# Modulation weights as 256 rows by 1024 columns, columns made by transposes, and low weights signalled in pieces

## The chip, the cores and the metric

The kernel runs on one core of one Trainium2 chip. The metric is the device time of one execution in microseconds (us). Engines are named as in the profile: PE is TensorE, DVE VectorE, ACT ScalarE, POOL GpSimd, SP SyncE, whose queue issues the loads of weights.

## The reference

The program is the whole forward pass of a trunk of two layers on 384 tokens: 128 tokens of a prompt and 256 latent tokens, each a vector of 1024 features. Layer 0 mixes tokens with HGRN2 and mLSTM, layer 1 with windowed attention and latent attention (MLA); each layer ends in a SwiGLU network with 2816 hidden features. All of it is fp32. Every layer is modulated by a condition: one vector for the prompt tokens (`c_ctx`) and one for the latent ones (`c`).

```python
def adaln(cond, w, b):
    m = jax.nn.silu(cond) @ w + b          # w: 1024 x 6144
    ...
    return jnp.split(m, 6, axis=-1)        # six vectors of 1024

for l in range(DEPTH):                     # once for the prompt with c_ctx, once for the latent tokens with c
    sh1, sc1, g1, sh2, sc2, g2 = adaln(cond, ada_w[l], ada_b[l])
    h = rms_norm(x, norm1_g[l]) * (1.0 + sc1) + sh1
    x = x + g1 * mixer(h)
    h = rms_norm(x, norm2_g[l]) * (1.0 + sc2) + sh2
    x = x + g2 * ((silu(h @ ffn_w1[l]) * (h @ ffn_w3[l])) @ ffn_w2[l])
```

The change is about the product with `ada_w`: two layers of 1024 x 6144 weights, 50.3 MB of the 162.43 MB that the kernel reads, for only two condition vectors. It gives twelve vectors of 1024 values.

## The kernel before

Activations lie with features on the 128 partitions, in eight tiles, and 384 tokens along the free axis. Every weight matrix is cut into units of up to 1 MB by `plan_units`. SP loads them in that order into a ring of three slots (`raw`, RAW=3): before the load of unit u it waits until unit u-3 is released. A unit of an ordinary matrix is then split into a high and a low part: ACT writes `w_hi` (L1084, up to 2048 columns in one instruction) and POOL writes `w_lo = raw - w_hi` (L1060, pieces of 512 columns), two buffers of each. POOL signals `lo_ready` once for a unit. PE then makes three products for each k-tile, high by high, low by high and high by low (L434 to L436 in `three`, L474 to L476 in `tokens`), 24 for an output tile of 1024 input features. `features` makes one output tile, `first_features` two at a time while the normalised input comes in tile by tile (`h_ready`).

Units of `ada_w` are not split. There are 48 of them, each all eight k-tiles by 256 columns; two make a pair of 512 columns, and there are 24 pairs. PE sums a unit in `strips` (L508): four strips of 32 partitions of a PSUM bank, strip g with k-tiles g and g+4. When both units of a pair are in, DVE copies 128x512 from PSUM (L1506, `ada_row`), PE's `columns_to` (L521) makes columns of it with four small matmuls against the constant `strips`, which also add up the four strips, and DVE adds the bias (L1494). The banks are a ring of two (`adas`). Columns of a pair are made by PE when the next pair has been summed.

Where the pairs are summed is written out by hand in `ADA_PLACES`: four at the start, one in the levels stage of HGRN2 (place norm0, in two halves at j=9 and j=10), one ahead of mLSTM (hgrn_norm), four in mLSTM behind steps j=0 to 3, one ahead of mLSTM's norm, one in norm1 ahead of layer 0's FFN, ten in that FFN (loaded by ACT's queue into a buffer of its own, `vada_raw`), one in norm2, one in norm3. In a norm, DVE's `norm(n, base, place)` writes the tiles `ht` (L1533), and at tile 0 it takes the pair of that place, so that it waits for PE's strips there.

In the levels stage (j = 6 to 17) PE makes one unit of `in0` for each j, and `level` products (L633) behind it. In cq, in layer 1, PE turns the cache with `turn(misc, ("cache",), ...)` and waits on `cq_ready` for the query compression that DVE splits (`cq_lo`), then multiplies by uq.

Of the kernel before, what the change touches and what calls it, by code (L numbers as in the profile page):

```python
# [56 lines left out]
for _name, _k in (("ident", 128), ("ones", 128), ("strips", 2), ("levels", 8 * 128),  # L57
                  ("tri_f", 128), ("tri_b", 128), ("big_f", 128), ("big_b", 128)):
    CONSTS[_name] = (_n, _k)
    _n += _k  # L60
# [8 lines left out]
def shape_constants():  # L69
# [9 lines left out]
    put("strips", np.tile(np.eye(32, 2, dtype=np.float32), (4, 1)))  # L79
    pos = np.arange(TL)  # L80
    rows, cols = (pos // 64).astype(np.float32), (pos % 64).astype(np.float32)
    for name, d, n in (("swa", 64, 2), ("mla", 32, 4)):
# [4 lines left out]
        for a, at in ((0, rows), (1, cols)):  # L87
# [4 lines left out]
            for i in range(half):  # L92
# [33 lines left out]
def ada_pairs(place):  # L126

    at = 0
    for name, n in ADA_PLACES.items():
        if name == place:  # L130
            return range(at, at + n)
        at += n
    raise KeyError(place)


def plan_units():
# [31 lines left out]
    add("in1", 1, DT, 160, 5)  # L168
    add("uq", 2, 3, 384)
# [3 lines left out]
    add("up1", 2, DT, 256)  # L173
    ada("norm3")
    add("up1", FT - 2, DT, 256, 2)
# [4 lines left out]
def build(nc, I, O):  # L180
# [9 lines left out]
    with ctx:  # L190
# [17 lines left out]
        ada_row = sb("ada_row", [P, 2, 512])  # L208
# [169 lines left out]
        first_vada = ada_pairs("ffn0")[0]  # L378
# [38 lines left out]
        vada_at_up = {3 * q + 5: q for q in range(VADA_UP // 2)}  # L417
        vada_at_down = {min(2 * q + 2, DT - 1): VADA_UP // 2 + q for q in range((VADA - VADA_UP) // 2)}

        @block.tensor  # L420
        def _(pe):
            def raw_unit(u):

                pe.wait_ge(raw_in[u % RAW], raw_need[u])
                return raw[u % RAW][:, 0:2048].rearrange("p (k n) -> p k n", k=DT)

# [12 lines left out]
            def unit_ready(u):  # L439
                pe.wait_ge(S["lo_ready"], split_index[u] + 1)  # L440

            def features(key, u, c, k_tiles=DT, x=(h_hi, h_lo), n=T):

                out = dense.fill(pe, key)[:, 0:n]
                unit_ready(u)
                three(out, [(*weight(u, k_tiles, k, c), x[0][:, k, 0:n], x[1][:, k, 0:n]) for k in range(k_tiles)])\
                    .then_inc(dense.done, 1)
                release[u] = (dense.done, dense.at[key] + 1)

            def first_features(keys, u, ready):  # L450

                outs = [dense.fill(pe, key)[:, 0:T] for key in keys]
                unit_ready(u)
                for k in range(DT):
                    pe.wait_ge(S["h_ready"], ready + k + 1)
# [6 lines left out]
            def tokens(key, u, c, n, chunk, k_tiles=DT, x=(h_hi, h_lo), out=None, more=False, last=True):  # L462
# [3 lines left out]
                unit_ready(u)  # L466
# [6 lines left out]
                for j, (s_hi, s_lo, m_hi, m_lo) in enumerate(terms):  # L473
                    pe.matmul(bk[:, at:at + n], s_hi, m_hi, start=j == 0, stop=False)  # L474
# [15 lines left out]
            def vada_half(n):  # L490

                p = first_vada + n // 2
                if n % 2 == 0:
                    vada_out[0] = adas.fill(pe, ("ada", p))
                pe.wait_ge(vada_in[n % 2], 16 * (n // 2 + 1))
                mm = strips(vada_out[0], n % 2, vada_raw[:, n % 2, :].rearrange("p (k n) -> p k n", k=DT))
                if n % 2:
# [3 lines left out]

            vada_out = [None]

            def strips(out, i, w):

                for k in range(DT):
                    g = k % 4
# [1508 lines left out]
```

## Time and profile before

| | |
|---|---|
| three runs | 1201.55, 1201.96 and 1206.5 us (median 1201.96) |
| profiled execution | 1202.52 us, its span 1200.7 us, mean granted clock of PE 0.953 |
| PE, DVE, ACT, POOL busy | 1110.2, 437.6, 399.0, 541.8 us |
| waits of PE's modulation strips on `ada_w` loads | 27.5 us in 13 waits |
| read from HBM | 162.43 MB, 138 GB/s over the span |

The times in the views are microseconds from the start of the span, those in the groups nanoseconds where they are means. Busy is the time in which an engine executes; the chain is followed back from the last instruction, at each step to what released it, so a row in it is time that the end waited for. A pipelined matmul shows some 0.34 us although the next one starts 0.17 us behind it.

### The profile page before, as it was taken

The numbers are of one execution on the slowest core, as the hardware profiler recorded it, in microseconds if no ns is written. First come the engines' busy times: TensorE is split into PE (matmuls) and PEld (weight loads), VectorE is DVE, ScalarE is ACT, GpSimd is POOL, SyncE is SP. The second block draws the span as 40 slices with busy tenths as digits, with TensorE's granted clock in tenths as the row PEclk, the third lists the DMA queues.
The fourth block names the chain that finished last, engine by engine and source line by source line (L and its number), as shares of the span: only waits on it lengthen the run. The fifth ranks groups of instructions, "written<-read, shape, count | busy, mean of one in ns | idle before, by whom it ended". The sixth has DMA issues, their size and how long they took to land.

```text
span 1200.7 us, 17368 instructions
## 1 busy us (share of the span) xinstructions
PE 1110.2 (92%) x7181; PEld 1022.6 (85%) x7181; DVE 437.6 (36%) x886; ACT 399.0 (33%) x617; POOL 541.8 (45%) x422
## 2 busy tenths in 40 slices
PE   5799999978789999999999799779998999999997
PEld 3599999966679999999999698655697999999997
DVE  4647899138563111111112310457465111111122
ACT  0532332434234322223212333456424232332221
POOL 0355478350063555554555433211053656565662
PEclk9799999979799999999999899879998999999998
DMA  9633443458336666664667711231034444534441
GB/s 309 198 108 106 142 141 105 151 180 284 88 117 176 199 195 191 176 185 131 196 188 199 229 42 38 67 86 51 1 103 128 121 135 110 141 98 135 122 121 53
DMA packets 243018, 166.47 MB, mean 139 GB/s; under 512 B 20269, under 2 KB 241532, under 8 KB 242812
## 3 DMA queue, kind: packets, MB, share of 16 engines
q1 hardware_dynamic: 214880, 135.74, 39.2%
q10 hardware_dynamic: 28060, 29.63, 7.8%
q8 instruction: 57, 0.93, 0.3%
q14 instruction: 21, 0.17, 0.0%
HBM read 162.43 MB, written 2.92 MB: 138 GB/s over the span
## 4 chain that ended last, share of the span: by engine, by line
PE 78%; DVE 7%; DMA 5%; POOL 3%; ACT 3%; issue 1%; ACTq 0%; SPq 0%; DVEq 0%
PE banks L434 20%; PE banks L436 20%; PE banks L435 20%; DMA raw<-in_ada_w 4%; PE banks L508 3%; POOL w_lo L1060 3%; PE banks L474 2%; PE banks L475 2%; PE banks L476 2%; DVE ht L1533 2%; PE banks L633 2%; DVE h_lo L1524 2%; ACT w_hi L1084 1%; PE banks L521 1%; PE banks L487 1%
## 5 line engine op out<-in xcount | busy, mean ns | idle before, releaser
L1060 POOL TENSOR_TENSOR w_lo<-raw,w_hi 128x512 fp32r<-128x512 f32 (+2 forms) x410 | 535.0, 1336 | 630.0 <-ACT w_hi L1084 629.9
L434 PE MATMUL banks<-h_hi,w_hi 128*128 128x384 f32 x1088 | 373.8, 344 | 20.7 <-DVE h_lo L1524 11.5
L435 PE MATMUL banks<-h_lo,w_hi 128*128 128x384 f32 x1088 | 368.3, 339 | 0.0
L436 PE MATMUL banks<-h_hi,w_lo 128*128 128x384 f32 x1088 | 368.3, 339 | 0.0
L1084 ACT ACTIVATE w_hi<-raw 128x2048 fp32r<-128x2048 f32 (+4 forms) x115 | 193.5, 1683 | 244.1 <-PE banks L436 172.1
L434 PEld LDWEIGHTS banks<-h_hi,w_hi 128*128 128x128 f32 x1088 | 207.4, 191 | 33.0 <-issue 29.3
L435 PEld LDWEIGHTS banks<-h_lo,w_hi 128*128 128x128 f32 x1088 | 207.6, 191 | 0.6
L436 PEld LDWEIGHTS banks<-h_hi,w_lo 128*128 128x128 f32 x1088 | 207.1, 190 | 0.6
L1587 DVE TENSOR_TENSOR uf<-sa,banks 128x384 f32<-128x384 f32 x44 | 24.4, 554 | 330.2 <-PE banks L436 324.3
L434 PE MATMUL banks<-u_hi,w_hi 128*128 128x384 f32 x352 | 119.8, 340 | 1.0 <-POOL w_lo L1060 1.0
L436 PE MATMUL banks<-u_hi,w_lo 128*128 128x384 f32 x352 | 118.3, 336 | 0.0
L435 PE MATMUL banks<-u_lo,w_hi 128*128 128x384 f32 x352 | 118.3, 336 | 0.0
L1571 DVE SCALAR_TENSOR_TENSOR X<-banks,mod,X 128x128 f32<-128x128 f32 x64 | 23.8, 413 | 193.9 <-PE banks L436 193.8
L1148 ACT ACTIVATE u_hi<-uf 128x384 fp32r<-128x384 f32 x44 | 23.1, 525 | 183.8 <-DVE uf L1587 183.8
L434 PEld LDWEIGHTS banks<-u_hi,w_hi 128*128 128x128 f32 x352 | 66.2, 188 | 4.5 <-issue 2.9
L435 PEld LDWEIGHTS banks<-u_lo,w_hi 128*128 128x128 f32 x352 | 66.2, 188 | 0.0
L436 PEld LDWEIGHTS banks<-u_hi,w_lo 128*128 128x128 f32 x352 | 66.2, 188 | 0.0
L508 PE MATMUL banks<-raw,cond 128*32 128x256 f32 x448 | 36.8, 461 | 27.5 <-DMA raw<-in_ada_w 27.5
L474 PE MATMUL banks<-w_hi,h_hi 128*128 128x256 f32 (+1 forms) x216 | 61.3, 284 | 0.0
L475 PE MATMUL banks<-w_lo,h_hi 128*128 128x256 f32 (+1 forms) x216 | 60.9, 282 | 0.0
L476 PE MATMUL banks<-w_hi,h_lo 128*128 128x256 f32 (+1 forms) x216 | 60.9, 282 | 0.0
L508 PEld LDWEIGHTS banks<-raw,cond 128*32 128x32 f32 x448 | 13.7, 124 | 45.2 <-DMA raw<-in_ada_w 28.4
(311 smaller groups left out, 1204.5 us busy)
## 6 DMA issues: line engine op xcount, KB each, us to landing
raw<-in_ffn_w SPq DMA_DIRECT2D x88, 512.0 KB, 5.2
raw<-in_ada_w SPq DMA_DIRECT2D x28, 1024.0 KB, 7.3
raw<-in_ffn_w SPq DMA_DIRECT2D x32, 704.0 KB, 4.6
vada_raw<-in_ada_w ACTq DMA_DIRECT2D x20, 1024.0 KB, 6.6
raw<-in_w_in_even SPq DMA_DIRECT2D x18, 1024.0 KB, 5.3
raw<-in_w_out_even SPq DMA_DIRECT2D x4, 1024.0 KB, 5.5
raw<-in_w_in_odd SPq DMA_DIRECT2D x3, 1024.0 KB, 7.2
raw<-in_w_in_odd SPq DMA_DIRECT2D x8, 256.0 KB, 4.3
```

The costliest lines, as they stand in the source:

```text
L434: pe.matmul(out, s_hi, m_hi, start=first and j == 0, stop=False)
L435: pe.matmul(out, s_hi, m_lo, start=False, stop=False)
L436: mm = pe.matmul(out, s_lo, m_hi, start=False, stop=last and j == len(terms) - 1)
L474: pe.matmul(bk[:, at:at + n], s_hi, m_hi, start=j == 0, stop=False)
L475: pe.matmul(bk[:, at:at + n], s_hi, m_lo, start=False, stop=False)
L476: mm = pe.matmul(bk[:, at:at + n], s_lo, m_hi, start=False, stop=j == k_tiles - 1)
L508: mm = pe.matmul(out[32 * g:32 * g + 32, 256 * i:256 * i + 256], cond[:, k, :], w[:, k, :], start=i == 0 and k < 4, stop=k >= 4, skip_grou ...
L633: mm = pe.matmul(out[:, h * P:(h + 1) * P], k_side[:, h, c * P:(c + 1) * P], q_side[:, h, c * P:(c + 1) * P], start=h == 0, stop=h == H - ...
L1060: ins = pool.tensor_tensor(w_lo[s % SPLIT][:, at:to], raw[u % RAW][:, at:to], w_hi[s % SPLIT][:, at:to].bitcast(F32), ALU.subtract)
L1084: act.activation(w_hi[s % SPLIT][:, 0:n], raw[u % RAW][:, 0:n], ACT.Copy)\
L1524: ins = dve.scalar_tensor_tensor(h_lo[:, m, a:b], ht[:, m % 2, a:b], mod[:, l, 8 * k + m, c:c + 1], h_hi[:, m, a:b].bitcast(F32), ALU.add, ...
L1587: dve.tensor_tensor(uf[:, f % 2, :], sa[:, f % 2, :], bk[:, 0:T], ALU.mult)\
```

## The change

A unit of `ada_w` becomes 256 rows by 1024 columns, that is two k-tiles by a whole vector; it has rows of 4 KB in memory where it had rows of 1 KB. Four units make a vector. Strip g now sums the columns 256 g to 256 g + 255 over all eight k-tiles, so no strips are left to be added: DVE copies 128x256, two transposes make columns (32 per strip, of which two are used), and one DVE instruction adds the bias to sixteen values. The constant `strips` goes.

POOL raises `lo_ready` behind every piece. `unit_ready(u, k)` makes PE wait for as many pieces as k-tile k needs, when more are needed than it has already seen; SP waits for the count of the whole unit.

Places are counted in units. The pair ahead of mLSTM moves into levels, which then has four units at j=9 to 12 and completes a vector. The vector that norm2 begins is completed in a new place cq, between the turned cache and the wait on `cq_ready`; norm3 has no units any more, and norm2 no longer holds up DVE. The columns of the last mLSTM vector are made before the strips of mlstm_norm.

```diff
-ADA_PLACES = {"start": 4, "norm0": 1, "hgrn_norm": 1, "mlstm": 4, "mlstm_norm": 1, "norm1": 1, "ffn0": 10,
-              "norm2": 1, "norm3": 1}
-assert sum(ADA_PLACES.values()) == 24
-VADA, VADA_UP = 2 * ADA_PLACES["ffn0"], 12
+ADA_PLACES = {"start": 8, "levels": 4, "mlstm": 8, "mlstm_norm": 2, "norm1": 2, "ffn0": 20, "norm2": 2, "cq": 2}
+assert sum(ADA_PLACES.values()) == 48
+VADA, VADA_UP = ADA_PLACES["ffn0"], 12
...
-    def ada(place, pairs=None):
-        units.extend((f"ada{p // 12}", 2 * (p % 12) + i, DT, 256)
-                     for p in (ada_pairs(place) if pairs is None else pairs) for i in range(2))
-    ada("start", range(0, 3))
+    def ada(place, first=0, end=None):
+        units.extend((f"ada{n // 24}", n % 24, 2, 1024) for n in ada_units(place)[first:end])
+    ada("start", 0, 6)
     add("in0", 1, DT, 256)
-    ada("start", range(3, 4))
+    ada("start", 6)
     add("in0", 6, DT, 256, 1)
     add("gates", 1, DT, 16)
-    first, second = [(f"ada{p // 12}", 2 * (p % 12) + i, DT, 256) for p in ada_pairs("norm0") for i in range(2)]
     add("in0", 2, DT, 256, 7)
-    units.append(first)
-    add("in0", 1, DT, 256, 9)
-    units.append(second)
-    add("in0", 8, DT, 256, 10)
+    for i in range(4):
+        ada("levels", i, i + 1)
+        add("in0", 1, DT, 256, 9 + i)
+    add("in0", 5, DT, 256, 13)
     add("out0", 2, DT, 256)
-    for place in ("hgrn_norm", "mlstm", "mlstm_norm"):
+    for place in ("mlstm", "mlstm_norm"):
...
+    ada("cq")
...
-    ada("norm3")
...
+        vada_at_up = {f + 1: n // 4 for f, n in VADA_AT_UP.items() if n % 4 == 3}
+        vada_at_down = {min(m + 1, DT - 1): n // 4 for m, n in VADA_AT_DOWN.items() if n % 4 == 3}
+        lo_need = [0]
+        for u in split_units:
+            lo_need.append(lo_need[-1] + (units[u][2] * units[u][3] + 511) // 512)
...
-            def unit_ready(u):
-                pe.wait_ge(S["lo_ready"], split_index[u] + 1)
+            lo_seen = [0]
+            def unit_ready(u, k=None):
+                s, n = split_index[u], units[u][3]
+                need = lo_need[s + 1] if k is None else lo_need[s] + (n * (k + 1) + 511) // 512
+                if need > lo_seen[0]:
+                    pe.wait_ge(S["lo_ready"], need)
+                    lo_seen[0] = need
             def features(key, u, c, k_tiles=DT, x=(h_hi, h_lo), n=T):
                 out = dense.fill(pe, key)[:, 0:n]
-                unit_ready(u)
-                three(out, [(*weight(u, k_tiles, k, c), x[0][:, k, 0:n], x[1][:, k, 0:n]) for k in range(k_tiles)])\
-                    .then_inc(dense.done, 1)
+                for k in range(k_tiles):
+                    unit_ready(u, k)
...
+            def strips(out, i, w):
+                for k in range(2):
+                    for g in range(4):
+                        mm = pe.matmul(out[32 * g:32 * g + 32, 0:256], cond[:, 2 * i + k, :], w[:, k, 256 * g:256 * g + 256],
+                                       start=i == 0 and k == 0, stop=i == 3 and k == 1, skip_group_check=True)
+                return mm
...
                     out = adas.fill(pe, ("mod", p))
                     adas.was_read(pe, ("ada", p))
-                    for j in range(4):
-                        mm = pe.matmul(out[:, 2 * j:2 * j + 2], ada_row[:, p % 2, j * P:j * P + P], cst("strips"),
-                                       start=j == 0, stop=True, skip_group_check=True)
-                    mm.then_inc(adas.done, 1)
+                    for j in range(2):
+                        tr = pe.transpose(out[:, j * P:j * P + P], ada_row[:, p % 2, j * P:j * P + P], ident)
+                    tr.then_inc(adas.done, 1)
...
+            def modulation(place, first=0, end=None, between=None):
+                for n in ada_units(place)[first:end]:
+                    u = number[(f"ada{n // 24}", n % 24)]
+                    pe.wait_ge(raw_in[u % RAW], raw_need[u])
+                    mm = strips(ada_bank(n), n % 4, raw[u % RAW][:, 0:2048].rearrange("p (k n) -> p k n", k=2))
+                    if n % 4 < 3:
+                        mark(mm, ("ada", n))
+                        release[u] = (S["half_used"], marks[("ada", n)])
+                    else:
+                        mm.then_inc(adas.done, 1)
+                        release[u] = (adas.done, adas.at[("ada", n // 4)] + 1)
+                        columns_to(n // 4)
+                    if between is not None:
+                        between()
+                        between = None
...
-                        columns_to(first_vada if l == 0 else 24)
+                        columns_to(first_vada if l == 0 else 12)
...
             for j in range(6, 18):
-                if j in (9, 10):
-                    modulation_half(ada_pairs("norm0")[0], j - 9)
+                if 9 <= j < 13:
+                    modulation("levels", j - 9, j - 8)
...
-            modulation("hgrn_norm")
...
-                modulation("mlstm", ada_pairs("mlstm")[j:j + 1])
+                modulation("mlstm", 2 * j, 2 * j + 2)
                 for i in TURN_HEADS.get(j, ()):
                     turn_head(i)
+            columns_to(5)
             modulation("mlstm_norm")
...
+            modulation("cq")
             pe.wait_ge(S["cq_ready"], 3)
...
-            modulation("norm3", between=lambda: stat(3))
+            stat(3)
...
-                        sp.wait_ge(S["lo_ready"], split_index[last] + 1)
+                        sp.wait_ge(S["lo_ready"], lo_need[split_index[last] + 1])
...
+                elif name[:3] == "ada":
+                    pieces_of = [(dst, k_first(w[name])[:, i % 4 * 2:i % 4 * 2 + 2, i // 4 * D:i // 4 * D + D])]
...
-                ins.then_inc(S["lo_ready"], 1)
+                    ins.then_inc(S["lo_ready"], 1)
...
-                    dve.tensor_tensor(mod[:, l, t:t + 4, :], bk[:, 0:8].rearrange("p (j c) -> p j c", c=2),
-                                      ada_b_col[:, 48 * l + t:48 * l + t + 4].unsqueeze(2).to_broadcast([P, 4, 2]),
+                    dve.tensor_tensor(mod[:, l, t:t + 8, :].rearrange("p (g j) c -> p j g c", j=2),
+                                      bk[:, 0:256].rearrange("p (j g w) -> p j g w", j=2, g=4)[:, :, :, 0:2],
+                                      ada_b_col[:, 48 * l + t:48 * l + t + 8].rearrange("p (g j) -> p j g", j=2)
+                                      .unsqueeze(3).to_broadcast([P, 2, 4, 2]),
                                       ALU.add).then_inc(adas.read(("mod", p)), 1)
...
+            def take_rows(p):
+                bk = adas.filled(dve, ("ada", p))
+                if ("mod", p - 2) in adas.at:
+                    adas.filled(dve, ("mod", p - 2))
+                dve.tensor_copy(ada_row[:, p % 2, :], bk[:, 0:256]).then_inc(adas.read(("ada", p)), 1)
+                biases_to(p)
+            def modulation(place, first=0, end=None):
+                for n in ada_units(place)[first:end]:
+                    if n % 4 == 3:
+                        take_rows(n // 4)
...
-                    if place is not None:
-                        modulation(place, ada_pairs(place)[m:m + 1])
+                    if place is not None and m == 0:
+                        modulation(place)
...
+            biases_to(5)
             gains(1)
...
-            norm(2, 24, "norm2")
+            norm(2, 24, None)
...
             rope(5)
+            modulation("cq")
...
-            norm(3, 32, "norm3")
+            norm(3, 32, None)
```

## Rows read from the trace of the kernel before

**Rows 1.** The page, chain that ended last: shares of the span by engine.
```profile
PE 78%; DVE 7%; DMA 5%; POOL 3%; ACT 3%; issue 1%; ACTq 0%; SPq 0%; DVEq 0%
```

**Rows 2.** Waits of PE: line, released by: us in total, times, longest.
```profile
PE banks L508 <- DMA raw<-in_ada_w: 27.5, 13, 8.0
...
PE banks L434 <- POOL w_lo L1060: 6.5, 5, 4.3
...
PE banks L434 <- DVE cq_lo L1924: 3.5, 1, 3.5
```

**Rows 3.** Groups by shape: busy us, mean ns | idle before, releasers.
```profile
L434 PE MATMUL banks<-u_hi,w_hi 128*128 128x384 f32 x352 | 119.8, 340 | 1.0 <-POOL w_lo L1060 1.0
...
L521 PE MATMUL banks<-const,ada_row 128*128 128x2 f32 x192 | 26.2, 259 | 1.6 <-DVE ada_row L1506 1.6
...
L1506 DVE COPY ada_row<-banks 128x512 f32<-128x512 f32 x24 | 16.5, 689 | 35.5 <-PE banks L508 26.7 <-issue 7.4 <-DVE PX L1827 0.7
```

**Rows 4.** Chain in order of time, the start: start us, us, what.
```profile
21.73 5.71 DMA raw<-in_ada_w
...
29.47 7.87 DMA raw<-in_ada_w
...
38.46 2.41 PE banks L521 x16
...
54.65 4.96 POOL w_lo L1060 x4
```

**Rows 5.** Windows: busy by engine, granted clock, DMA share, GB/s.
```profile
10.00:15.00 5.00, 2.25 (x20) 0.60 (x16) 0.69 (x1) 0.00 (x0) 0.00 (x0) 1.00 1.04 389
30.00:35.00 5.00, 4.44 (x14) 2.53 (x18) 2.58 (x6) 3.34 (x3) 1.39 (x2) 0.50 1.10 349
280.00:285.00 5.00, 3.75 (x46) 2.90 (x39) 3.12 (x12) 1.00 (x3) 0.00 (x0) 1.00 1.09 350
```

**Rows 6.** GpSimd's groups by shape, 150 to 205 us, then 360 to 660.
```profile
L1060 POOL TENSOR_TENSOR w_lo<-raw,w_hi 128x512 fp32r<-128x512 f32 x21 | 45.1, 2178 | 19.3 <-ACT w_hi L1084 19.2
...
L1060 POOL TENSOR_TENSOR w_lo<-raw,w_hi 128x512 fp32r<-128x512 f32 x111 | 140.5, 1295 | 147.6 <-ACT w_hi L1084 147.6
```

**Rows 7.** Chain in order of time, levels stage.
```profile
144.42 1.00 PE banks L508 x16
...
179.59 2.68 PE banks L633 x24
191.03 2.68 PE banks L633 x24
```

**Rows 8.** Chain in order of time, mLSTM stage.
```profile
268.99 6.50 DMA raw<-in_ada_w
...
280.32 7.98 DMA raw<-in_ada_w
...
290.40 1.06 PE banks L487 x9
...
306.36 3.43 PE banks L508 x32
```

**Rows 9.** Chain in order of time, FFN of layer 0 and norm2.
```profile
373.68 1.91 ACT w_hi L1084
...
416.74 0.79 PE banks L521 x8
...
671.98 9.24 DMA raw<-in_ada_w
...
685.04 0.75 DVE ht L1533 x2
```

**Rows 10.** Timeline of PE at the first down products.
```profile
573.60 0.44 PE L434 MATMUL banks<-u_hi,w_hi 128*128 128x384 f32 x1 [0.57 <-POOL w_lo L1060]
573.88 0.34 PE L435 MATMUL banks<-u_lo,w_hi 128*128 128x384 f32 x1
574.06 0.34 PE L436 MATMUL banks<-u_hi,w_lo 128*128 128x384 f32 x1
```

More of the change, by code:

```diff
@@ L56 @@
 _n = 0
-for _name, _k in (("ident", 128), ("ones", 128), ("strips", 2), ("levels", 8 * 128),
+for _name, _k in (("ident", 128), ("ones", 128), ("levels", 8 * 128),
                   ("tri_f", 128), ("tri_b", 128), ("big_f", 128), ("big_b", 128)):
@@ L78, in shape_constants @@
     put("ones", np.ones((P, P), np.float32))
-    put("strips", np.tile(np.eye(32, 2, dtype=np.float32), (4, 1)))
     pos = np.arange(TL)
@@ L500, in vada_half @@
                     mm.then_inc(S["vada_half"], 1)
[L502 to L507, printed above, removed]
-                    mm = pe.matmul(out[32 * g:32 * g + 32, 256 * i:256 * i + 256], cond[:, k, :], w[:, k, :],
-                                   start=i == 0 and k < 4, stop=k >= 4, skip_group_check=True)
-                return mm
             columns_made = [0]
@@ L602, in _ @@
             misc.was_read(pe, "cond")
-            modulation("start", range(0, 1))
+            modulation("start", 0, 2)
             pe.wait_ge(S["x_in"], 32)
@@ L615, in _ @@
             pe.matmul(out[:, 0:32], ones[0:1, :], row_in[:, :], start=True, stop=True).then_inc(misc.done, 1)
-            modulation("start", range(1, 3))
+            modulation("start", 2, 6)
             stat(0)
-            modulation("start", range(3, 4))
-            columns_to(4)
+            modulation("start", 6)
+            columns_to(2)
             in0 = lambda c: (number[("in0", c // 256)], c % 256)
@@ L892, in scores @@
                     pe.wait_ge(S["roped"], 8)
-                    adas.was_read(pe, ("ada", ada_pairs("norm2")[-1]))
+                    adas.was_read(pe, ("ada", 11))
                     dense.was_read(pe, ("vm", 3))
@@ L1498, in biases_to @@
                     biases_made[0] += 1
-            def modulation(place, pairs=None):
-                for p in (ada_pairs(place) if pairs is None else pairs):
-                    bk = adas.filled(dve, ("ada", p))
-                    if ("mod", p - 2) in adas.at:
-                        adas.filled(dve, ("mod", p - 2))
-                    dve.tensor_copy(ada_row[:, p % 2, :], bk[:, :]).then_inc(adas.read(("ada", p)), 1)
-                    biases_to(p)
+            def take_rows(p):
[6 more added lines that the diff above has]
+                for n in ada_units(place)[first:end]:
+                    if n % 4 == 3:
+                        take_rows(n // 4)
             def gains(n):
@@ L1591, in ffn @@
                     if l == 0:
-                        if f in VADA_AT_UP and VADA_AT_UP[f] % 2:
-                            p = first_vada + VADA_AT_UP[f] // 2
-                            modulation("ffn0", range(p, p + 1))
+                        if f in VADA_AT_UP and VADA_AT_UP[f] % 4 == 3:
+                            take_rows(first_vada + VADA_AT_UP[f] // 4)
                         if f in vada_at_up:
@@ L1605, in ffn @@
                         take_y(m - 1)
-                    if l == 0 and VADA_AT_DOWN[m] % 2:
-                        p = first_vada + VADA_AT_DOWN[m] // 2
-                        modulation("ffn0", range(p, p + 1))
+                    if l == 0 and VADA_AT_DOWN[m] % 4 == 3:
+                        take_rows(first_vada + VADA_AT_DOWN[m] // 4)
                     if l == 0 and m in vada_at_down:
@@ L1615, in _ @@
             dve.memset(cond[:, :, :], 0.0).then_inc(S["cond_clear"], 1)
-            modulation("start", range(0, 1))
+            modulation("start", 0, 2)
             for c in range(NCH):
@@ L1629, in _ @@
             step(dve.tensor_scalar(neg_sink[:, :], rowb[:, 0:8], -1.0, None, ALU.mult))
-            modulation("start", range(1, 2))
+            modulation("start", 2, 4)
             dense.was_read(dve, ("x", NCH - 1, 1))
@@ L1633, in _ @@
                 add_squares(0, m)
-            modulation("start", range(2, 4))
-            biases_to(4)
+            modulation("start", 4)
+            biases_to(2)
             gains(0)
@@ L1771, in _ @@
                 ins.then_inc(misc.read(("kv", 2 + d)), 1)
-            modulation("norm0")
+            modulation("levels")
             bk = dense.filled(dve, "m_cols")
@@ L1860, in _ @@
             weights(0)
-            modulation("hgrn_norm")
             dve.wait_ge(S["hg_sq"], 1)
@@ L1869, in _ @@
                 finish(j)
-                modulation("mlstm", ada_pairs("mlstm")[j:j + 1])
+                modulation("mlstm", 2 * j, 2 * j + 2)
                 if j == 0:
```

91 lines of the change are left out of this document (31 added, 60 removed).

## The prediction

> **What bounds the kernel now.** I read the page's chain that ended last first: the matrix engine holds 78 % of it, VectorE 7 %, DMA 5 %, GpSimd and ScalarE 3 % each, so a change pays where it takes matmuls off TensorE's stream or ends one of its waits [rows 1]. The waits of PE say which are within reach of this diff: 27.5 us of the modulation strips (L508) wait on loads of `ada_w`, the largest wait of all, 6.5 us of feature matmuls on `w_lo`, in five waits, and 3.5 us at one place on `cq_lo` [rows 2]. Then the groups by shape give the price of each small operation [rows 3], and the chain in order of time shows which of these waits ended last in each stage [rows 4, 7 to 9]. Elsewhere PE streams fp32r matmuls 0.17 us apart [rows 10], and only work taken out of the stream counts there.
>
> **The sum**, stage by stage, against the profiled execution (1202.5 us, 1.8 above its span, 0.5 above the median of the runs).
>
> *Start.* Eight strip units are still loaded and summed. What changes: the chain ends its modulation with 16 column matmuls of 2.41 us [rows 4]; of these two vectors leave four transposes, half of which can run earlier. A transpose in the stream costs about 0.12 us at the full clock (nine in 1.06 us [rows 8]), double at the halved clock that is granted here (0.50 [rows 5]): I take 0.7 for what is left, -1.7; bounds -1.2 and -2.1. The loads of 5.71 and 7.87 us are chain [rows 4], at 349 GB/s; the same engines moved the 4 KB rows of the input tokens at 389 [rows 5]. If rows of 4 KB do that here too, 13.6 us of loads lose 10 %, -1.3 (bounds 0 and -1.4). Together **-3.0** (-1.2 to -3.5).
>
> Here a rule of the Trainium skill speaks against the last step. "DMA: Bandwidth & Descriptors", section Specifications, puts the least size for the line rate at 512 B and the HBM's share of a core near 358 GB/s: by it rows of 1 KB lose nothing against rows of 4 KB, and the 349 would already be the limit. The 389 of this trace disagrees, though the token rows follow one another in memory and the new pieces do not; it is rival C.
>
> *Second unit of in0.* PE stood still 4.3 us, its longest wait on `w_lo` [rows 2], while GpSimd made four pieces in 4.96 us [rows 4]. The signal now comes a piece (1.24 us) at a time, and a piece holds two k-tiles of a column tile: six matmuls, 6 x 0.174 = 1.04 us. PE therefore runs at GpSimd's pace and ends its first 24 matmuls one piece's work (1.04) behind the last piece instead of 24 x 0.174 = 4.18 behind it: -3.1, and at best the whole standstill goes, -4.3. I stay near the pace: **-3.5**.
>
> *Levels (j = 6 to 17).* Two units at j=9 and 10 become four at j=9 to 12. Two more strip units are 2 x 1.00 us in the stream [rows 7]. Worse is the ring of three `raw` slots: unit u waits for the release of u-3, so the load of in0's unit 11, which stood behind a split unit and could start early, now stands behind the strips of j=10, and unit 12's, which stood behind those, behind the strips of j=11. From there it is serial: load about 6 us (5.71 and 6.50 at other places [rows 4, 8]), `w_hi` 1.91 [rows 9], then four pieces. A piece takes 2.18 us here against 1.295 in the FFN [rows 6], so 8.7 us for the unit. PE's step of j is 11.44 us (from one `level` product to the next [rows 7]). The last piece lands 6 + 1.9 + 8.7 = 16.6 after the strips; PE wants it a step later, for the last quarter of its first 24 matmuls, 11.44 + 0.75 x 4.18 = 14.6: 2 us late if pieces take their mean, 4 if they take 2.7, once; the next unit then meets PE's delayed pace. Pieces give back about 1 us of the wait for a whole unit. **+4.5** (+2, strips alone, to +8, if the lateness comes at both units). Cover for the first part is only PE's own step.
>
> *mLSTM.* The pair at its start has moved into levels, so eight units of `ada_w` are loaded where there were ten. PE's chain here is load after load: 6.50 and 7.98 us at 269 and 280, with DMA at 350 GB/s [rows 5, 8]. A megabyte at 349 takes 3.0 us, so two fewer are -6.0; the eight left gain 10 % if long rows are faster, -2.4; a set of columns, 0.79 at the full clock [rows 9], shrinks to two transposes, 0.25, and comes twice where it came five times, -3.4 at most if none of it is hidden, of which I count -1. Not all can be had: once loads stop being last, the states' own products on VectorE and ScalarE are. I take **-8.0** (-5.5 to -9.4). At the end the two mlstm_norm units are still 32 matmuls (3.43 us [rows 8]), but the gains no longer want the last pair's copy and columns behind them (0.69 [rows 3] + 0.79 and the bias, some 0.2 to 0.4): **-1.8**, 0 if VectorE is late with the heads' sums there, -1.9 at best.
>
> *norm1.* VectorE still waits on the strips; its copy falls from 128x512 (0.69 [rows 3]) to half the columns (between 0.35 and 0.69; I take 0.42) and a bias addition behind it goes: **-0.6** (0 to -0.9).
>
> *FFN of layer 0.* Strips are as many: twenty units of 16 records. Nine times the stream holds column matmuls of 0.79 us [rows 9]; four times two transposes (0.25) remain: -6.1, and in a stage where PE is never idle it is all kept. At f=1 the first column set (0.79 to 0.25) and a wait on `w_lo` (the five waits of 6.5 us less the 4.3 leave some 0.55 for each [rows 2], one shown as 0.57 [rows 10]) go: -1.1. At the entry to the down products another 0.57: in all **-7.8** (-6.0 to -8.6).
>
> *norm2.* Its unit's load, 9.24 us, is chain, and behind its strips VectorE, which stood at tile 0 of `ht` until they were summed, takes 1.44 us for each of the other tiles (six rows that far apart) [rows 9], where PE needs six matmuls a tile, 1.04: 7 x 0.4 = 2.8 us of waits, and some 2 us from strips to the first tile. Now `norm` takes no place and the tiles run on during the load. What becomes last is the load itself, which PE's first features still follow, perhaps at a lower clock after that wait. **-3.5** (-1 to -5).
>
> *cq.* Two strip units now stand just ahead of `cq_ready`, on which PE waited 3.5 us anyway [rows 2]: their 2.0 us are hidden, and are lost where that wait is gone. But on SyncE's queue they stand ahead of uq, uk, uv and out1, whose loads now wait for these strips through the ring, while ScalarE's split of uq's second unit and GpSimd's of uv come later. The nearest row is a wait on `w_lo` as those of [rows 2], between nothing and 3 us. **+0.4** (0 to +3).
>
> *norm3 and the FFN of layer 1.* The copy and bias go from VectorE's first tile (-0.8), f=1 and the down entry as above (-1.1, -0.6): **-2.5** (-1 to -2.9).
>
> Sum: -3.0 -3.5 +4.5 -8.0 -1.8 -0.6 -7.8 -3.5 +0.4 -2.5 = -25.8. From 1202.5: **1177**. With all the bad bounds about -7 (1196), with all the good ones -34 (1168).
>
> **Rivals.** A measurement of this kernel tells about 0.5 % (6 us) from no change.
>
> A, *the moves give it back.* Levels cost the whole +8 because both loads come late, mLSTM yields 3 us because VectorE's chain paces it, and the end of mLSTM nothing: 3.5 + 5.0 + 1.8 worse, 1187; with norm2 at -1, 1189.5. For it: GpSimd's slow pieces in levels [rows 6]. Against: mLSTM's waits on DMA are the longest of the 27.5 [rows 2, 8]. 0.22.
>
> B, *the new waits cost.* By the plan of units, 44 of up, 18 of in0 and some 16 of out and in1 have four pieces and 32 of down have three: about 295 pieces beyond the first, and as many possible waits in the middle of accumulations. A late wait costs its idle time and a slow restart: the matmul after 573.60 comes 0.28 us behind it and the next 0.18, so 0.11 at most [rows 10]. At 0.11 for each wait +32 us: 1209, slower. It decides from 0.09 us a wait (25.8/295). Against it: the down products of m=0 already wait on `u_ready` at every k-tile, and 352 matmuls of that form have 1.0 us of idle time in all, every bit of it on `w_lo` [rows 3]. 0.06.
>
> C, *long rows load no faster*: the 349 GB/s are what scattered rows of any length get, and the 389 belong to tokens that lie in one piece [rows 5]. Then 1.3 at the start and about 2 in mLSTM are lost: 1180. 0.15; whether it holds, the loads' landing times tell.
>
> **Chances and range.** The sum as it stands 0.52 (its own range 1171 to 1183), C 0.15, A 0.22, B 0.06; the rest, 0.05, is a gain larger than the good bounds or a stall not seen. A is faster than the half per cent unless several bad bounds meet, which I put at a quarter of it, 0.06, within it; all but 0.01 of B is slower. Faster 0.87, within 0.07, slower 0.06. The range leaves out B, A's worst part and the far good end: 1166 to 1194.
>
> **What the changed profile would show.** Twenty-four transposes in place of 192 column matmuls, twelve copies of 128x256. No idle of 4 us before the second unit of in0. In levels PE waits on GpSimd or on loads at j=11 and 12, a few us in all. Loads of `ada_w` landing 10 % sooner at the start (C: not). The stretch from the first mLSTM strips to out0 about 10 us shorter, with waits on DMA fallen from 27.5 to about 12. FFN of layer 0 about 8 shorter, that of layer 1 about 2. VectorE's `ht` tiles of norm2 unbroken, and PE waiting no longer than now ahead of uq. The prediction fails if matmuls of features space out at k = 2, 4, 6 (B), if the levels stage grows by much over 5, or if mLSTM keeps its length with PE waiting on VectorE.

## The result, and the profile after

The changed kernel takes 1168.95 us (median of four runs, 1168.46 to 1170.17) against 1202.16 before: a ratio of 0.9716, interval 0.9696 to 0.9736. That is 33 us less, where 25.5 were forecast. Five more runs, beside the last experiments, gave 1168.97. The profiled execution took 1168.79 us with a span of 1166.3; the mean granted clock rose from 0.953 to 0.969.

The page of the changed kernel, its chain by engine [rows 1]:

```profile
PE 81%; DVE 8%; DMA 4%; ACT 3%; POOL 2%; issue 1%; ACTq 1%; SPq 0%; DVEq 0%
```

Its waits of PE [rows 2]. L495 is now the strips, L427 the first product of three, L1053 the low weights:

```profile
PE banks L495 <- DMA raw<-in_ada_w: 27.1, 9, 8.8
PE banks L427 <- DVE h_lo L1524: 14.6, 7, 6.7
...
PE banks L427 <- POOL w_lo L1053: 2.4, 3, 1.1
```

The waits on `w_lo` fell from 6.5 to 2.4 us, and the one on `cq_lo` is no longer among the long ones. The waits on loads of `ada_w` did not fall, 27.5 to 27.1: there are fewer of them, and the longest is 8.8 us where it was 8.0. The groups by shape [rows 3]:

```profile
L1500 DVE COPY ada_row<-banks 128x256 f32<-128x256 f32 x12 | 5.1, 422 | 8.9 <-PE banks L495 6.7 <-issue 1.9 <-DVE PX L1827 0.2
L526 PE MATMUL banks<-const,ada_row 128*128 128x128 f32 x24 | 5.1, 294 | 1.6 <-DVE ada_row L1500 1.6
```

Twelve copies of 0.42 us and 24 transposes stand where there were 24 copies of 0.69 and 192 small matmuls. The chain in order of time, at the places that answer to [rows 4, 7 to 9]:

```profile
33.14 3.25 PE banks L495 x32
38.13 0.76 DVE ht L1533 x2
...
51.22 1.28 POOL w_lo L1053
...
160.00 2.68 PE banks L637 x24
163.12 1.00 PE banks L495 x16
172.66 2.68 PE banks L637 x24
...
247.28 9.80 POOL w_lo L1053 x8
257.51 8.51 DMA raw<-in_ada_w
...
293.82 0.90 PE banks L488 x3
...
334.57 1.92 ACT w_hi L1077
...
379.81 1.00 PE banks L495 x16
...
653.28 0.76 DVE ht L1533 x2
```

At the start the strips run straight into `ht`, without the 2.41 us of columns; one piece of low weights (1.28) is in the chain where four (4.96) were; in levels one step is 12.66 us, the old 11.44 and a strip unit, with no stall in it; ahead of mLSTM the chain runs through eight pieces of low weights and a load of 8.51 us, where it ran through four pieces and a load of 5.14. Matching events of the two traces, by their starts, give the time of each stage:

| from one event to the next | before | after | difference | forecast |
|---|---|---|---|---|
| span's start to `ht` of norm0 | 41.58 | 38.13 | -3.45 | -3.0 |
| to the 48 `level` products | 70.23 | 65.53 | -4.70 | -3.5 |
| to the last `level` products | 79.22 | 81.66 | +2.44 | +4.5 |
| to the three transposes ahead of mlstm_norm's strips | 114.43 | 108.50 | -5.93 | -8.0 |
| to the split of up0's second unit (`w_hi`, ahead of norm1) | 45.15 | 40.75 | -4.40 | -1.8 |
| to the FFN's first strips | 47.08 | 45.24 | -1.84 | -1.7 |
| to its last strips | 260.21 | 252.71 | -7.50 | -6.7 |
| to the squares of cq (six matmuls) | 85.01 | 81.09 | -3.92 | -3.5 |
| to the split of uv's second unit | 34.99 | 34.92 | -0.07 | +0.4 |
| to the split of up1's second unit (ahead of norm3) | 119.38 | 118.05 | -1.33 | 0 |
| to the last residual additions | 293.02 | 289.28 | -3.74 | -2.5 |
| all of these | | | -34.44 | -25.8 |

The two ends of the deviation are mLSTM, 2 us short, and levels and the stage behind mLSTM, together 4.7 us better than forecast. The experiments look for these, and for what each part gives.

### The profile page after: what moved, and what is told of

Same layout as the page of the kernel before. It is cut to its first block, busy times and chain, and to the rows that moved or that the text cites. A ratio compares the mean times of both kernels' runs of the same rounds, so it can differ in the third digit from the quotient of the medians.

```text
span 1166.3 us, 16906 instructions
## 1 busy us (share of the span) xinstructions
PE 1076.7 (92%) x7013; PEld 989.8 (85%) x7013; DVE 424.2 (36%) x862; ACT 398.7 (34%) x617; POOL 533.1 (46%) x422
## 4 chain that ended last, share of the span: by engine, by line
PE 81%; DVE 8%; DMA 4%; ACT 3%; POOL 2%; issue 1%; ACTq 1%; SPq 0%; DVEq 0%
PE banks L427 22%; PE banks L428 21%; PE banks L429 21%; PE banks L495 3%; PE banks L475 2%; PE banks L477 2%; DVE ht L1533 2%; PE banks L476 2%; PE banks L637 2%; DVE h_lo L1524 2%; DMA raw<-in_ada_w 1%; POOL w_lo L1053 1%; PE banks L488 1%; PE banks L929 1%; DMA E<-m_rows 1%
## 5 line engine op out<-in xcount | busy, mean ns | idle before, releaser
L1053 POOL TENSOR_TENSOR w_lo<-raw,w_hi 128x512 fp32r<-128x512 f32 (+2 forms) x410 | 525.3, 1312 | 602.5 <-ACT w_hi L1077 602.5
L427 PE MATMUL banks<-h_hi,w_hi 128*128 128x384 f32 x1088 | 370.6, 341 | 19.1 <-DVE h_lo L1524 14.6
L427 PEld LDWEIGHTS banks<-h_hi,w_hi 128*128 128x128 f32 x1088 | 205.5, 189 | 32.3 <-issue 29.4
L427 PE MATMUL banks<-u_hi,w_hi 128*128 128x384 f32 x352 | 119.5, 339 | 0.0
L427 PEld LDWEIGHTS banks<-u_hi,w_hi 128*128 128x128 f32 x352 | 66.0, 188 | 2.9 <-issue 2.9
L495 PE MATMUL banks<-raw,cond 128*32 128x256 f32 x448 | 38.1, 478 | 27.2 <-DMA raw<-in_ada_w 27.1
L495 PEld LDWEIGHTS banks<-raw,cond 128*32 128x32 f32 x448 | 14.2, 130 | 45.0 <-DMA raw<-in_ada_w 28.9
```

The source lines that it names most:

```text
L427: pe.matmul(out, s_hi, m_hi, start=first and j == 0, stop=False)
L495: mm = pe.matmul(out[32 * g:32 * g + 32, 0:256], cond[:, 2 * i + k, :], w[:, k, 256 * g:256 * g + 256], start=i == 0 and k == 0, stop=i == ...
L1053: ins = pool.tensor_tensor(w_lo[s % SPLIT][:, at:to], raw[u % RAW][:, at:to], w_hi[s % SPLIT][:, at:to].bitcast(F32), ALU.subtract)
```

## The experiments

Each is timed beside runs of the kernel before on the same chip; the changed kernel's 1168.95 is the level for those that start from it. The kernel before took 1201.9 to 1203.7 us in these sets, so medians of different sets that lie 2 or 3 us apart do not settle a matter; there the stages of the traces have to.

**Without pieces** (e_whole), and **pieces alone** (e_pieces_alone). The first waits for the whole unit:

```diff
-                need = lo_need[s + 1] if k is None else lo_need[s] + (n * (k + 1) + 511) // 512
+                need = lo_need[s + 1]
```

> The changed kernel, but TensorE waits for all pieces of a unit before its first matmul, as before the change. My theory (pieces pay where TensorE stands at the head of a unit): the standstill ahead of in0's second unit comes back (+4.7 us, what that stage lost between the two traces) and about 0.55 at each of four FFN entries: +7, so 1176 us. Rival 1, pieces pay at the start alone, the FFN entries being held by ScalarE and VectorE anyway: +5, 1174. Rival 2, the waits in the middle of accumulations cost something each: this kernel then loses less than 4, below 1173.

The second puts the counts, the waits for each k-tile and the signal for each piece into the kernel before, and nothing else:

```diff
-                unit_ready(u)
                 for k in range(DT):
+                    unit_ready(u, k)
...
-                ins.then_inc(S["lo_ready"], 1)
+                    ins.then_inc(S["lo_ready"], 1)
```

> The kernel before with the signal in pieces and nothing else of the change. My theory: in0's second unit -4.7 us and -0.55 at each of four FFN entries, -7, so 1195 us. Rival 1, the start alone: -5, 1197. Rival 2, the waits in the middle of accumulations cost: 1199 or more. If the gains of the parts add, this gain is that which e_whole loses; if the granted clock ties the parts together (what one part leaves idle lowers the clock for another) the two differ.

Measured: e_whole 1183.33 us (ratio 0.9835, 0.9795 to 0.9875), 14.4 over the changed kernel; pieces alone 1190.07 (0.9912, 0.9892 to 0.9931), 11.8 under the 1201.86 beside it. I had expected 7 us of each, so both gains are near twice that, and the new waits cost nothing that can be seen: rival B falls. The waits of PE in e_whole:

```profile
PE banks L427 <- POOL w_lo L1053: 11.3, 6, 4.6
```

By the starts of ScalarE's splits, e_whole loses 4.7 us at in0, 1.4 behind f=1 of the FFN, 0.9 at its down entry, 3.2 around uq (46.0 us from the split of uq's first unit to that of uv's second, against 42.8), 1.3 behind f=1 of layer 1, 0.8 at its down entry, and 2.0 inside layer 1's FFN, where each step takes 8.42 us and not 8.32. Another 0.9 lie between the splits of out0's second and third unit, but there PE waits for no low weights in any of these traces; out0 begins at a lower clock in e_whole, of which more below. The loss inside the FFN is seen in two windows of 84 us of that FFN, here e_whole, then the changed kernel:

```profile
938.00:1022.00 84.00, 84.00 (x480) 82.54 (x479) 10.24 (x20) 27.99 (x31) 50.19 (x41) 1.00 0.45 125
```

```profile
925.00:1009.00 84.00, 84.00 (x486) 84.00 (x485) 10.23 (x20) 28.24 (x30) 51.22 (x42) 1.00 0.46 126
```

PE is busy all of both windows at the full clock, yet 486 matmuls fit where 480 did. In e_whole the first product of a unit there starts up to 0.30 us behind the one before it and the second 0.25; in the changed kernel all are 0.17 apart. The wait at the head of a unit hides in this spacing and never shows as idle time. A ledger of waits from the trace alone misses it. The trace of pieces alone shows the same places: in0 4.7, layer 1's FFN 2.0, but at uq only 0.8; out0 is no faster in it (36.0 us with and without pieces). The parts add up: 20.4 (e_whole under the 1203.74 beside it) and 11.8 are 32.2, the whole change 33.

**The pair back ahead of mLSTM** (e_pair_back): two units in levels, two at mLSTM's start.

```diff
-                if 9 <= j < 13:
+                if 9 <= j < 11:
                     modulation("levels", j - 9, j - 8)
...
             states(0)
+            modulation("hgrn_norm")
```

> The changed kernel with two of the four units of the levels stage moved back ahead of mLSTM, as the pair lay before the change. My theory (mLSTM is a queue of loads, 3 us each): levels 2.4 us shorter, mLSTM 6 longer, +3.6, so 1172.5 us. Rival: the long wait of 8.8 us ahead of mLSTM's first strips is the time of another unit's slot, not of the number of loads, and two more units are hidden by it or by VectorE's chain behind: -2.4 to 0, so 1166.5 to 1169.

Measured: 1173.38 us (0.9743, 0.9714 to 0.9772), 4.4 over the changed kernel; its interval overlaps that of the changed kernel, so the traces say more than the medians. There levels are 2.4 us shorter and the time up to out0's first product 5.4 longer (5.0 by the table's stage of mLSTM). My account of the move holds, nearly to the number: 2 x 1.2 against 2 x 2.7 us.

**Runs of 1 KB against 4 KB** (e_rows1k, e_rows4k). Each unit of `ada_w` on SyncE's queue is loaded in two transfers, one for each k-tile; only the order of blocks in the slot differs, and with it the length of the runs in a transfer; in memory the values lie as before: `g k n` below is e_rows1k, `k g n` in its place is e_rows4k.

```diff
+                    to = raw[u % RAW][:, 0:2048].rearrange("p (g k n) -> p k g n", g=4, k=2)
+                    pieces_of = [(to[:, k], k_first(w[name])[:, i % 4 * 2 + k, i // 4 * D:i // 4 * D + D].rearrange("p (g n) -> p g n", g=4))
+                                 for k in range(2)]
```

> The changed kernel with each unit of ada_w on SyncE's queue loaded as two transfers (one for each k-tile) whose rows are cut into runs of 1 KB by the layout of the slot; TensorE reads the same values. To be compared with e_rows4k, which has the same two transfers in runs of 4 KB. My theory (runs of 4 KB load some 10 % faster): the start +1.3 and mLSTM +2 over e_rows4k, about +3.3 us, the rate in the saturated stretches back at 349 GB/s. Rival C (no difference between runs of 1 and of 4 KB): within 0.5 us of e_rows4k.

> The changed kernel with each unit of ada_w on SyncE's queue loaded as two transfers in runs of 4 KB, the control of e_rows1k. Both theories: one more issue of about 0.4 us for a unit on a queue that mostly waits, 0 to +1 us over the changed kernel, 1169 to 1170.

Measured: 1175.59 us (0.9762, 0.9732 to 0.9792) with runs of 1 KB, 1169.32 (0.9713, 0.9688 to 0.9737) with 4 KB: 6.3 us, about twice what I expected, for 28 loads. The intervals touch, but every run of the one lies above every run of the other. Windows in mLSTM (the last columns are granted clock, DMA share, GB/s), e_rows1k:

```profile
265.00:270.00 5.00, 3.83 (x36) 2.96 (x39) 2.82 (x9) 1.07 (x4) 0.00 (x0) 0.81 1.10 353
270.00:275.00 5.00, 3.83 (x48) 2.48 (x40) 3.85 (x14) 2.71 (x10) 0.00 (x0) 1.00 1.10 348
```

and e_rows4k:

```profile
260.00:265.00 5.00, 3.52 (x37) 2.74 (x35) 2.82 (x9) 1.13 (x4) 0.00 (x0) 0.96 1.02 401
265.00:270.00 5.00, 4.22 (x32) 3.41 (x32) 1.86 (x5) 2.54 (x10) 0.00 (x0) 0.73 1.01 391
```

At a full DMA share the runs of 1 KB move 348 to 353 GB/s, those of 4 KB 391 to 401, some 13 % more; rival C falls. In the traces the start up to in0's second unit is 3.6 us longer with short runs, mLSTM 2.6, norm2 1.0; out0 is 1.6 us longer with long ones, by its clock (below).

**A wait of VectorE in norm2** (e_norm2_wait): at tile 0 it waits for norm2's second unit.

```diff
+                    if n == 2 and m == 0:
+                        dve.wait_ge(S["half_used"], marks[("ada", ada_units("norm2")[1])])
```

> The changed kernel, but at tile 0 of norm2 VectorE waits until TensorE has summed norm2's second unit, as it did before the change; nothing is copied there. My theory: the tiles behind it come 1.44 us apart again behind the load, +3.5 us, 1172.5 (norm2's stage lost 3.9 between the traces). Rival: the load itself and the first tile are what TensorE waits for, and the shorter copy and columns ahead of norm2 made the difference: below +1, 1169 to 1170.

Measured: 1171.06 us (0.9751, 0.9732 to 0.9771), 2.1 over the changed kernel, with overlapping intervals; its trace has 1.9 in that stage. It lies between the two theories. VectorE's timeline in this run, whose second `ht` tile comes behind the strips:

```profile
654.40 0.75 DVE L1533 SCALAR_TENSOR_TENSOR ht<-X,gain,rstd 128x128 f32<-128x128 f32 x2 [5.08 <-ACT rstd L1102]
656.94 0.75 DVE L1533 SCALAR_TENSOR_TENSOR ht<-X,gain,rstd 128x128 f32<-128x128 f32 x2 [1.79 <-PE banks L495]
```

The wait is 1.79 us and nothing more: behind it tiles come 1.44 us apart, but so they do without it (`ht` at 655.68, 657.12, 658.56 in the changed kernel). I had counted that spacing as a price of the wait; it is VectorE's own pace.

**The masks behind out0's first unit** (e_mask_later), a step to find what held mLSTM:

```diff
-            masked_after = {split_index[number[("in0", 17)]]: (0, 2 * H)}
+            masked_after = {split_index[number[("out0", 0)]]: (0, 2 * H)}
```

> The changed kernel with one line of GpSimd's order changed: the masks of mLSTM's weights, which wait for a load of rows from memory (landing at 239.5 us), stand behind the low weights of out0's first unit instead of ahead of them. My theory of the term that fell short (mLSTM gave 5.9 us where 8.0 were counted): the second mLSTM unit of ada_w waits for the slot of out0's first unit, whose low weights stand behind those masks, so TensorE's wait of 8.8 us ahead of the first strips is that order and not the rate of loads. Then the wait shrinks to about 0 to 2 and the kernel gains 3 to 8 us: 1161 to 1166. Rival, mLSTM is bound by the sum of its loads or by VectorE: the wait moves to the next units, and the gain is under 1.5: 1167.5 to 1169.

Measured: 1165.95 us (0.9699, 0.9683 to 0.9715), 3.0 under the changed kernel, the low end of my theory; the intervals overlap, and in the traces mLSTM is 3.6 us shorter. GpSimd's timeline in the changed kernel, then in this one:

```profile
239.57 5.80 POOL L1043 TENSOR_TENSOR PFSI<-PFSI,const 128x384 f32<-128x384 f32 x6 [13.42 <-DMA E<-m_rows]
245.30 1.98 POOL L1043 TENSOR_TENSOR E<-E,const 128x384 f32<-128x384 f32 x2
247.23 9.84 POOL L1053 TENSOR_TENSOR w_lo<-raw,w_hi 128x512 fp32r<-128x512 f32 x8
```

```profile
232.82 5.05 POOL L1053 TENSOR_TENSOR w_lo<-raw,w_hi 128x512 fp32r<-128x512 f32 x4 [5.84 <-ACT w_hi L1077]
239.80 5.79 POOL L1043 TENSOR_TENSOR PFSI<-PFSI,const 128x384 f32<-128x384 f32 x6 [1.93 <-DMA E<-m_rows]
```

GpSimd stood idle for 13.42 us behind a load of rows that the masks need, with eight pieces of out0 queued behind it, and the slot of those pieces was what the second mLSTM unit waited for. With the order changed the second unit's strips run without a wait, and PE's wait of 8.83 us becomes 3.96 and 1.66 ahead of the third and the fourth, not the 0 to 2 that I had put. I took the rest for the slot of out0's second unit, which e_order below puts to the test.

**Four more units in levels** (e_levels8): one strip unit at each j from 9 to 16, one at each of mLSTM's first four steps.

```diff
-                if 9 <= j < 13:
+                if 9 <= j < 17:
                     modulation("levels", j - 9, j - 8)
...
-                modulation("mlstm", 2 * j, 2 * j + 2)
+                if j == 0:
+                    columns_to(4)
+                modulation("mlstm", j, j + 1)
```

> The changed kernel with four more units moved from mLSTM into levels (one at each j from 9 to 16, so one unit at each of mLSTM's first four steps). My theory: levels +1.2 for each unit, +4.9, with no stall since the four that are there stalled nothing; mLSTM's wait ahead of its first strips stays, and of the loads behind it 3 to 6 us are saved: 1167 to 1171, no real difference. Rival, mLSTM is bound by the number of loads: four fewer at 3 us each are -12, with +4.9: 1162.

Measured: 1170.47 us (0.9743, 0.9728 to 0.9758), 1.5 over the changed kernel, with overlapping intervals: where my theory put it, but not by its way. Levels cost 6.4 us and not 4.9, and out0 begins at the lower clock in its trace, which costs 1.6 (below). Its waits of PE:

```profile
PE banks L495 <- DMA raw<-in_ada_w: 14.7, 6, 4.8
...
PE banks L526 <- DVE ada_row L1503: 9.1, 3, 7.5
```

The wait on loads is halved, and in its place PE waits 7.5 us for a copy that I had put behind VectorE's first step of mLSTM. What four more units are worth without that wait was not tried.

**One unit of out0 ahead of mLSTM** (e_order), on top of the masks' new place:

```diff
-    add("out0", 2, DT, 256)
+    add("out0", 1, DT, 256)
     for place in ("mlstm", "mlstm_norm"):
         ada(place)
-    add("out0", 2, DT, 256, 2)
+    add("out0", 3, DT, 256, 1)
...
-            split_to(split_index[number[("out0", 0)]] + SPLIT)
+            split_to(split_index[number[("out0", 0)]] + 1)
```

> The changed kernel with three lines of order changed: one unit of out0 instead of two is loaded and split ahead of mLSTM's units of ada_w, and mLSTM's masks stand behind its low weights on GpSimd. So three units of ada_w can be in their slots before TensorE's first strips. My theory (what is left of mLSTM's wait, 4.0 and 1.7 us with the masks behind alone, is the slots taken by out0's second unit): no wait ahead of the first strips, 6 to 9 us less than the changed kernel, 1160 to 1163. Rival (behind the first strips the sum of the loads or VectorE takes over): no better than the masks alone, 1165 to 1167.

Beside it **cq's units behind uq** (e_cq, and e_order_cq on top of e_order), and the changed kernel again:

```diff
-    ada("cq")
     add("uq", 2, 3, 384)
+    ada("cq")
```

> The kernel of e_order with the two units of place cq loaded behind both units of uq instead of ahead of them. My theory: the second unit of uq is loaded some 15 us earlier and TensorE's waits on its low weights (1.10 and 0.38 us in the changed kernel) go: 1 to 2 us under e_order. Rival: ScalarE, which splits it only when it has done the split of cq, sets that time anyway: no difference.

> The changed kernel with the two units of place cq loaded behind both units of uq. My theory: 1 to 2 us under the changed kernel, 1167.5. Rival: no difference, 1169.

> The changed kernel as it is, beside the three that follow: 1169 us, within 2.

Measured: e_order 1158.51 us (0.9623, 0.9595 to 0.9651), 10.5 under the changed kernel's 1168.97 beside it, more than the 6 to 9 of my theory, and faster than both kernels. PE's timeline, the waits of strips in the changed kernel, then in e_order:

```profile
257.68 1.93 PE L495 MATMUL banks<-raw,cond 128*32 128x256 f32 x16 [8.83 <-DMA raw<-in_ada_w]
...
266.06 1.07 PE L495 MATMUL banks<-raw,cond 128*32 128x256 f32 x16 [1.84 <-DMA raw<-in_ada_w]
...
271.70 1.07 PE L495 MATMUL banks<-raw,cond 128*32 128x256 f32 x16 [1.64 <-DMA raw<-in_ada_w]
```

```profile
255.21 1.07 PE L495 MATMUL banks<-raw,cond 128*32 128x256 f32 x16 [0.44 <-DMA raw<-in_ada_w]
...
258.83 1.07 PE L495 MATMUL banks<-raw,cond 128*32 128x256 f32 x16 [0.62 <-DMA raw<-in_ada_w]
...
261.32 1.07 PE L495 MATMUL banks<-raw,cond 128*32 128x256 f32 x16 [1.42 <-DMA raw<-in_ada_w]
```

In the changed kernel the first unit's strips run without a wait and the second unit's wait 8.83 us; in e_order the first three run without one (249.0, 249.9 and 253.7). PE's waits on loads in mLSTM are 2.7 us in all, where they were 12.3. Behind 269 us the chain runs mostly through VectorE. e_cq took 1167.93 (0.9696, 0.9664 to 0.9727) and e_order_cq 1159.53 (0.9628, 0.9602 to 0.9654): no difference that can be measured, though the three waits on `w_lo`, 2.2 us in e_order, become one of 1.0 in e_order_cq. The second trace of the changed kernel has only one as well, without the edit. The rival holds there.

## Why the prediction was right, and by which terms

The sign, the range (1166 to 1194) and most stages came as forecast; the size came out 8.6 us short in the traces, by errors in both directions. Some 3.8 us of the 8.6 are the granted clock, at in0 and at out0, for which the sum had no term.

*Start.* The time was right (-3.45 for -3.0) and the split of it was not; that they agree is luck. The 3.6 us between e_rows1k and e_rows4k are all of the start's gain, where I had taken 1.3 for long runs and 1.7 for the columns: with short runs the loads come last and the columns were beside them.

*Pieces* were mis-sized: -3.5 at in0 and four times 0.55, 5.7 in all, against 11.8 alone and 14.4 in the changed kernel. I had priced them by the waits that the trace shows on `w_lo`. At in0 they gave 4.7 us, more than the 4.3 that I had as the best. PE's standstill there fell from 4.33 to 0.94 us; and behind it, in the kernel before, ten products start 0.30 to 0.32 us apart instead of 0.17, some 1.4 us in all, which the changed kernel does not have. Windows with the products behind the standstill, before, then after, whose first window also holds what is left of the standstill (the third last column is the granted clock):

```profile
60.00:65.00 5.00, 5.00 (x21) 5.00 (x21) 3.10 (x4) 0.00 (x0) 4.56 (x4) 0.66 0.68 210
```

```profile
51.00:56.00 5.00, 4.06 (x21) 3.33 (x21) 4.24 (x5) 4.20 (x6) 4.79 (x4) 1.00 0.52 161
56.00:61.00 5.00, 5.00 (x29) 4.75 (x29) 3.70 (x4) 0.49 (x1) 5.00 (x5) 1.00 0.66 210
```

The runs showed two more places: the uq products, and 0.1 us in each step of layer 1's FFN that lies in the spacing of matmuls. In cq the change's two units do make uq's second load late: e_whole loses 3.2 us around uq, pieces alone gain 0.8 there. My +0.4 came near the measured -0.07 because pieces take the lateness back, which I had not counted.

*Levels*: the two strip units cost 2.44, 1.22 each where I had 1.00; the lateness that I added, another 2, did not come, with pieces or without (e_whole has the same time there). In the changed kernel the 21 pieces between 150 and 205 us take 1.73 us each and not the 2.18 of [rows 6], the loads that follow the strips 5.2 to 5.3 us, and PE is busy through all of it. VectorE is busy 44.2 of these 55 us and was busy 53.7 of them in the old trace; whether that is why the pieces were slow there was not tested.

*mLSTM* is the step that failed: -8.0 for two loads fewer and faster ones, with PE's wait on loads to fall to about 12 in the whole kernel. It gave -5.9, and in mLSTM alone this wait rose from 10.7 to 12.3 us. The prices were right: e_pair_back shows that two loads are worth some 5 us there, and e_rows1k against e_rows4k that long rows are worth 2.6. What I had not seen, e_mask_later and e_order show. The wait ahead of the second unit's strips is the slots taken by out0's units, whose low weights stood behind masks that wait for a load. It stood in the chain of the kernel before, ahead of the loads that [rows 8] begins with:

```profile
234.62 8.89 DMA E<-m_rows
243.58 4.96 POOL PFSI L1050 x6
248.55 1.65 POOL E L1050 x2
250.19 4.94 POOL w_lo L1060 x4
255.15 5.14 DMA raw<-in_ada_w
```

and in that of the changed kernel:

```profile
228.92 10.57 DMA E<-m_rows
239.57 5.80 POOL PFSI L1043 x6
```

Taking units away does not touch it, and it was the largest single wait. It even grew: the load of rows and the masks took 2.8 us longer, so the second unit's strips start 72.4 us behind the last `level` products where they started 69.3 behind. That is as much as the missing 2.1 us and more. The load of rows takes 9.7 to 10.6 us in every trace of the changed kernel and of the experiments on it that has it in its chain, and 8.9 and 8.6 in the kernel before and with pieces alone; why it is longer is not shown.

*Behind mLSTM*: -4.4 where -1.8 was forecast. The first out0 products come 2.05 us sooner behind the last transposes, which is the term. The other 2.35 us lie inside out0, where no matmul was removed and PE waits for no low weights in either trace. They go with the granted clock: before, the first sixteen products start 0.32 us apart, after, 0.17. Windows over the first products of out0, before, then after:

```profile
314.00:318.00 4.00, 3.37 (x11) 3.40 (x12) 0.18 (x1) 0.00 (x0) 0.00 (x0) 0.50 0.93 231
```

```profile
300.00:304.00 4.00, 3.06 (x18) 3.09 (x19) 0.52 (x1) 0.00 (x0) 0.00 (x0) 1.00 1.06 329
```

The clock is at 1.2 GHz in the one (0.50) and at 2.4 in the other (1.00); a value between is a stretch that has both. Over all runs, out0 from its first product to the split of up0's second unit takes 33.6 us where the clock of the first 4 us is 1.00 (the changed kernel, e_pair_back, e_rows1k, e_norm2_wait, e_order, e_cq), 35.2 where it is 0.57 to 0.64 (e_whole, e_rows4k, e_mask_later, e_levels8), and 36.0 at 0.50 (before, pieces alone). So up to 2.4 us turn on what the clock does at one place, and e_mask_later lost there part of what it had gained. Ahead of out0 PE was busy 6.9 of 12 us in the changed kernel and 7.9 before; why the one began at the higher clock and the other at the lower is not shown.

*The columns* in the FFN of layer 0 and f=1: as forecast (-9.3 for -8.4), with pieces in the difference. *norm2*: -3.9 for -3.5, but only 1.9 of it by the wait taken from VectorE; the rest was not isolated, and the shorter load, copy and columns lie there. My sentence that the load becomes last was wrong: the chain runs through ScalarE's queue and `ht` at 653.28. *The attention's -1.3* had no term; the granted clock in the ten microseconds behind the uv products is 0.92 where it was 0.83, and this was not tested. The stage takes 117.0 to 120.1 us in the traces of the changed kernel and of the experiments on it, so 1.3 us lie within its spread.

## What to carry to other kernels

Signal a producer's output in pieces where the consumer walks through it in the same order: some 295 more waits cost PE nothing that can be seen, and the gain was twice what the visible waits added up to. When a wait on a transfer is the largest of a stage, ask first what holds its slot: here the order of the load queue, of ScalarE's splits and of GpSimd's masks, four lines, was worth 10.5 us, more than moving the loads; GpSimd's one line alone gave 3.0. A spacing read behind a wait is not the price of that wait until it is seen without it.

## What the runs showed of the hardware that was not expected

Saturated loads move 348 to 353 GB/s in runs of 1 KB and 391 to 401 in runs of 4 KB on the same matrix; it cost the kernel 6.3 us where I had expected 3.3. "DMA: Bandwidth & Descriptors" of the Trainium skill, section Specifications, lets the line rate begin at 512 B. The measurement differs from that and decides. The same section puts the HBM's limit for a core near 358 GB/s, as half of what a stack gives to two cores; with one core at work, as here, loads ran above it.

A stage with the same instructions took 33.6, 35.2 or 36.0 us by the clock that was granted at its start, and a standstill of 4.33 us was followed by ten products at nearly twice their spacing. And a wait for low weights of 0.1 us at the head of a unit showed as no idle time at all, but in the spacing of two matmuls.
